# Two-layer encoder trunk with routed experts: small loads placed elsewhere, expert matrices asked for in two steps

## The reference

```
h = RMSNorm(x) * (1 + scale1) + shift1            # scales from SiLU(c) @ ada_w
cols = h @ w_in                                   # split over four mixers A, B, C, D
x = x + gate1 * (concat(A, B, C, D) @ w_out)      # latent, windowed, differential attention, Hyena
h = RMSNorm(x) * (1 + scale2) + shift2
x = x + gate2 * HierMoE(h)
```

## Time and profile before

| | us |
|---|---|
| median of 3 runs | 1742.07 (1737.08 to 1742.08) |
| profiled execution, device time | 1743.41 |
| its span | 1741.6 |
| expert stage, layer 0: first gather issued to last asks after the loop | 574.2 to 862.9 |
| expert stage, layer 1: first gather issued to last result scaled | 1403.6 to 1676.9 |

### The profile page before, as it was taken

The page is one execution under the profiler, slowest core; times in us unless marked ns, Lnnn a source line. Parts: engine busy times, 40 slices in busy tenths (PEclk is TensorE's granted clock), DMA queues, the critical chain, the costliest instruction groups (busy, mean ns, idle before and its releaser), DMA issues.

```text
span 1741.6 us, 18433 instructions
## 1 busy us (share of the span) xinstructions
PE 1382.1 (79%) x6748; PEld 784.0 (45%) x6748; DVE 617.8 (35%) x1444; ACT 369.2 (21%) x832; POOL 266.7 (15%) x250
## 2 busy tenths in 40 slices
PE   2789999898696785888778999989869778877741
PEld 0245646565443443444424464656544344444420
DVE  3462523358624221222136152335761431111111
ACT  0311111545402110111021111154530211111101
POOL 0000310000001342333200030100000134333211
PEclk8799999999898798999978999999989879999976
DMA  7611120441335499999961112045124548999932
GB/s 237 256 46 49 73 88 17 152 176 43 126 124 229 172 286 359 405 404 406 346 241 60 49 63 98 1 147 191 49 105 146 230 161 323 402 402 404 396 134 109
DMA packets 98152, 335.53 MB, mean 193 GB/s; under 512 B 28310, under 2 KB 33046, under 8 KB 72816
## 3 DMA queue, kind: packets, MB, share of 16 engines
q1 hardware_dynamic: 74688, 305.48, 45.0%
q0 software_dynamic: 15072, 16.85, 4.4%
q10 hardware_dynamic: 8304, 12.03, 2.0%
HBM read 324.04 MB, written 27.80 MB: 202 GB/s over the span
## 4 chain that ended last, share of the span: by engine, by line
PE 63%; DVE 14%; issue 9%; ACT 7%; DMA 3%; POOL 2%; SPq 1%; POOLq 0%; DVEq 0%; ACTq 0%
PE bank L468 58%; ACT pr_r L1227 2%; PE bank L716 2%; PE bank L814 2%; DMA big<-in_ada_w_dram 1%; DVE pr_r L1833 1%; DVE pr_r L1694 1%; ACT pr_r L1274 1%; DVE pr_r L1836 1%; DVE pr_r L1559 1%; PE bank L566 1%; POOL small L1334 1%; ACT ht_r L1206 1%; SPq L927 1%; DVE small L1692 1%
## 5 line engine op out<-in xcount | busy, mean ns | idle before, releaser
L468 PE MATMUL bank<-big,pr_r 128*64 128x256 f32 (+2 forms) x3272 | 469.1, 407 | 103.0 <-issue 62.1
L468 PEld LDWEIGHTS bank<-big,pr_r 128*64 128x64 f32 (+1 forms) x3272 | 283.6, 153 | 261.1 <-issue 156.2
L468 PE MATMUL bank<-big,ht_r 128*128 128x512 f32 (+2 forms) x832 | 329.9, 547 | 1.5 <-ACT ht_r L1240 1.5
L468 PEld LDWEIGHTS bank<-big,ht_r 128*128 128x128 f32 x832 | 155.0, 190 | 144.4 <-issue 138.0
L468 PE MATMUL bank<-big 128*128 128x256 f32 (+4 forms) x528 | 191.7, 504 | 28.1 <-ACT big L1211 10.5
L1398 POOL DMA_INDIRECT x_rows<-ht_r,slot_i x64 | 101.7, 1590 | 359.2 <-DVE ht_r L1839 319.7
L468 PEld LDWEIGHTS bank<-big 128*128 128x128 f32 (+2 forms) x528 | 102.2, 205 | 86.1 <-issue 39.9
L1833 DVE TENSOR_TENSOR pr_r<-pr_r,bank 64x256 f32<-64x256 f32 x65 | 27.5, 423 | 291.4 <-ACT pr_r L1274 256.2
L1274 ACT ACTIVATE pr_r<-bank 64x256 f32<-64x256 f32 x64 | 24.1, 377 | 457.3 <-PE bank L468 426.8
L1839 DVE SCALAR_TENSOR_TENSOR ht_r<-bank,mix_r,mod 128x512 f32<-128x512 f32 x65 | 48.8, 751 | 135.9 <-PE bank L468 132.4
L1333 POOL TENSOR_SCALAR small<-small 128x1 f32<-128x1 f32 (+2 forms) x20 | 6.9, 346 | 574.9 <-DVE small L1719 326.6
(11 more groups left out here) (272 smaller groups left out, 1215.7 us busy)
## 6 DMA issues: line engine op xcount, KB each, us to landing
big<-in_moe_w_gate_dram SPq DMA_DIRECT2D x65, 1024.0 KB, 4.9
big<-in_moe_w_up_dram SPq DMA_DIRECT2D x65, 1024.0 KB, 6.9
big<-in_moe_w_down_dram SPq DMA_DIRECT2D x65, 1024.0 KB, 8.9
big<-in_ada_w_dram SPq DMA_DIRECT2D x16, 3072.0 KB
big<-in_w_in_dram SPq DMA_DIRECT2D x4, 3072.0 KB
big<-in_w_out_dram SPq DMA_DIRECT2D x4, 2048.0 KB
mod<-in_ada_b_dram SPq DMA_DIRECT2D x12, 512.0 KB, 5.5
big<-in_w_in_dram SPq DMA_DIRECT2D x2, 2048.0 KB
```

The lines of the kernel that those rows point to most:

```text
L468: return nc.tensor.matmul(o, l, r, start=start, stop=stop)
```

## The change

The loads of the vectors are split in groups with semaphores of their own. In layer 0, those of layer 1 are now issued so: `load_network` (weights, biases and frequencies of the filter network) and `load_conv` (conv weights and bias, the norm vectors, `k_lam`) before chunk 12 (the first half of w_out); `load_attention` (three broadcasts) at expert 2, after the mixers are done; `load_router` at expert 5; `load_filters`, now only its last four DMAs, and `load_mods` at expert 9 as before. Gate and up of expert e are asked for when the gate and up products of the expert before it in the slot are done, its down matrix when all of that expert's products are. The count is read at expert 24 on every engine.

```diff
+READ_AT = 24
...
@@ tensor, first filters of layer 0 (the same split in DVE's wait and at MLP_AT)
-                    pe.wait_ge(hy_in, 16 * 11)
+                    pe.wait_ge(net_in, 16 * 7)
+                    pe.wait_ge(hy_in, 16 * 4)
@@ tensor, before the experts
-                n_over = pe.value_load(tot_i[0:1, 0:1], min_val=0, max_val=EXTRA)
-                n_before = pe.value_load(tot_i[0:1, 1:2], min_val=0, max_val=EXTRA * DEPTH)
-
...
                 for e in range(NE):
                     expert(e)
+                    if e == READ_AT:
+                        n_over = pe.value_load(tot_i[0:1, 0:1], min_val=0, max_val=EXTRA)
+                        n_before = pe.value_load(tot_i[0:1, 1:2], min_val=0, max_val=EXTRA * DEPTH)
@@ sync
+            def load_network(l):
+                (hy_w1, hy_w2, hy_w3, hy_b1, hy_b2, hy_b3, hy_sin_freq: 7 DMAs on net_in)
...
+            def load_conv(l):
+                (hy_conv_w x3, hy_conv_b, mla_q_norm, mla_kv_norm, k_lam: 7 DMAs on vec_in)
...
+            def load_attention(l):
+                (diff_lambda, diff_norm_g, swa_sink: 3 DMAs on vec_in)
...
+            def load_router(l):
+                (router_g_b, router_e_b: 2 DMAs on vec_in)
@@ sync, the chunks of a layer
                     if n == 5:
                         load_late_mods(l)
+                    if CHUNKS[n] == ("out", 0) and l + 1 < DEPTH:
+                        load_network(l + 1)
+                        load_conv(l + 1)
                     chunk_used(sp, CHUNKS[n - 2])
                     load_chunk(n, l)
@@ sync, the experts
                 for e in range(NE):
                     s = EXPERT_SLOT[e]
+                    if e == 2 and l + 1 < DEPTH:
+                        sp.wait_ge(mix_ready, l + 1)
+                        load_attention(l + 1)
+                    if e == 5 and l + 1 < DEPTH:
+                        taken(sp, "lgT")
+                        load_router(l + 1)
                     if before_in_slot(e) is not None:
+                        sp.wait_ge(gu_done, NE * l + before_in_slot(e) + 1)
+                        load_first(e)
                         sp.wait_ge(y_done, NE * l + before_in_slot(e) + 1)
+                        load_down(e)
                     elif s < 2:
...
-                    load_expert(e)
-                    if e == 5:
+                    if before_in_slot(e) is None:
+                        load_first(e)
+                        load_down(e)
+                    if e == READ_AT:
                         taken(sp, "over")
...
                     if e == 9 and l + 1 < DEPTH:
                         load_filters(l + 1)
-                        load_vectors(l + 1)
                         load_mods(l + 1)
@@ scalar and gpsimd: the two value_loads at e == READ_AT, not at e == 4
@@ vector: the two value_loads after the result of expert READ_AT, not before the loop
```

More of the change, by code:

```diff
@@ L265, in trunk @@
         slot_full = [sem(f"slot_full{i}") for i in range(5)]
-        hy_in, vec_in = (sem(n) for n in "hy_in vec_in".split())
+        hy_in, net_in, vec_in = (sem(n) for n in "hy_in net_in vec_in".split())
         x_in = [sem(f"x_in{t}") for t in range(NT)]
@@ L852, in expert @@
                         else:
-                            pe.wait_ge(hy_in, 16 * 11 * (l + 2))
+                            pe.wait_ge(net_in, 16 * 7 * (l + 2))
+                            pe.wait_ge(hy_in, 16 * 4 * (l + 2))
                         mm(bank[4 + b][0:64, :], (hw1, hw2, hw3)[j], mlp_h if j else zT).then_inc(mlp_done, 1)
@@ L909, in load_chunk @@
                     sp.dma_start(at(big, s * SLOT, KT, m), src.rearrange("(p k) n -> p k n", k=KT)).then_inc(slot_full[s], 16)
-            def load_filters(l):
[L913 to L917, removed]
+            def load_network(l):
+                for w, name in ((hw1, "hy_w1"), (hw2, "hy_w2"), (hw3, "hy_w3")):
+                    sp.dma_start(w, of_layer(name, l)).then_inc(net_in, 16)
+                for j, name in enumerate(("hy_b1", "hy_b2", "hy_b3")):
+                    sp.dma_start(hb[:, j:j + 1], row_of(name, l).rearrange("a n -> n a")).then_inc(net_in, 16)
+                sp.dma_start(hf, of_layer("hy_sin_freq", l).rearrange("j n -> n j")).then_inc(net_in, 16)
+            def load_filters(l):
                 sp.dma_start(zT, a["k_z"]).then_inc(hy_in, 16)
@@ L957, in load_empty @@
                 sp.dma_start(slots_of.rearrange("(p n) o -> p (n o)", p=P), a["k_empty"]).then_inc(fill_in, 16)
+            load_network(0)
             load_filters(0)
@@ L962, in _ @@
             load_mods(0)
-            load_vectors(0)
+            load_attention(0)
+            load_conv(0)
+            load_router(0)
             load_chunk(1, 0)
@@ L974, in layer, with load_first @@
                         load_late_mods(l)
+                    if CHUNKS[n] == ("out", 0) and l + 1 < DEPTH:
+                        load_network(l + 1)
+                        load_conv(l + 1)
                     chunk_used(sp, CHUNKS[n - 2])
                     load_chunk(n, l)
-                def load_expert(e):
+                def load_first(e):
                     s = EXPERT_SLOT[e]
-                    wg, wu, wd = expert_slot(s)
+                    wg, wu, _ = expert_slot(s)
                     src = l * NE + TURN[e]
@@ L985, in load_expert, with load_down @@
                         "a (p k) f -> (a p) k f", k=KT)).then_inc(slot_full[s], 16)
-                    sp.dma_start(wd, a["moe_w_down"].rearrange("l e f d -> (l e) f d")[bass.ds(src, 1)].rearrange(
+                def load_down(e):
+                    s = EXPERT_SLOT[e]
+                    src = l * NE + TURN[e]
+                    sp.dma_start(expert_slot(s)[2], a["moe_w_down"].rearrange("l e f d -> (l e) f d")[bass.ds(src, 1)].rearrange(
                         "a (p j) d -> (a p) j d", j=2)).then_inc(slot_full[s], 16)
@@ L1274, in layer @@
                     A_(sil[0:CAP, b, :], bank[2 + b][0:CAP, 0:F], ACT.Silu).then_inc(silu_ready, 1)
-                    if e == 4:
+                    if e == READ_AT:
                         n_over = act.value_load(tot_i[0:1, 0:1], min_val=0, max_val=EXTRA)
@@ L1513, in mod_take @@
                         took(last)
-                v.wait_ge(hy_in, 16 * 11 * (l + 1))
+                v.wait_ge(net_in, 16 * 7 * (l + 1))
+                v.wait_ge(hy_in, 16 * 4 * (l + 1))
                 step(TS(bias_b, bias_b, 2.0 / (2 * S), None, ALU.mult))
@@ L1857, in layer @@
                     y_evac(e % 4, slot_w[:, TURN[e]:TURN[e] + 1]).then_inc(yg_ready, 1)
+                    if e == READ_AT:
+                        n_over = v.value_load(tot_i[0:1, 0:1], min_val=0, max_val=EXTRA)
+                        n_before = v.value_load(tot_i[0:1, 1:2], min_val=0, max_val=EXTRA * DEPTH)
                     if e in MLP_AT and l + 1 < DEPTH:
```

9 lines of the change are left out of this document (3 added, 6 removed).

## The result

The changed kernel takes 1731.09 us, median of 14 runs (1725.47 to 1736.71); the kernel before took 1742.07 (14 runs, 1736.74 to 1749.09; three of them, and its profile, were taken ahead of the prediction). The ratio is 0.9938, 95% interval 0.9924 to 0.9951: 11 us faster. The forecast said faster, by 19.5 us, 1723 with a range of 1713 to 1733. Sign and range held, the range near its slow end; the size was almost twice what came. The profiled execution took 1733.8 us, its span is 1732.0 (before: 1741.6).

What follows compares the result with a forecast made beforehand. The prediction took the DMA engines to bound the expert stages, so gains come from useless DMA time. Terms of 2.1, 9.9 and 7.5 us sum to 19.5 off 1743.41, stated as 1723 us, range 1713 to 1733.

Steps and rivals of the forecast that it cites:

- part 1: Start of both expert stages: removing PE's reads of the count saves 2.1 us in sum, bounds 0 and 2.75.
- in layer 0 I take 1.1, in layer 1 1.0: Before each stage's first transposes: of PE's 1.27 and 1.48 us issue waits, these amounts would be saved.
- Everything in the stage follows from these transposes: Start of each expert stage: the first transposes set all that follows, so the shorter wait counts as gain, 2.1 us.
- Part 2, the asks: Dry queue before expert 7, both layers: earlier gate and up asks gain 5.0 us a stage, 9.9 together, bounds 0 to 16.3.
- fits into the 7.6 us: Layer 0's hole before expert 7: 2.10 MB at 422 GB/s takes 5.0 us, within the 7.6 us by which the ask comes earlier.
- the stall goes too: Rival at expert 3, both layers: ACT's late SiLU start vanishes, the whole hole fills, 6.4 us more gain, 1717; chance 0.1.
- the page weighed against my rate: Refill of the holes: a 358 GB/s HBM bound would make it 5.9 us, worth 1.8 us more; 5.0 was kept.
- Part 3, the small loads: Layer 0, expert 9: moving small loads away from expert 10's asks saves 7.5 us, bounds 2.5 and 9.9.
- the rest, 7.6 us, is what the small loads cost: Layer 0's experts 9 to 31 take 15.7 us longer than layer 1's; remaining loads explain 8.1, moved ones the rest.
- Expert 10's gate and up are asked for by 642: SP in layer 0: with eight loads left at expert 9, the ask comes before 642, with 3.2 MB still queued.
- The cover of chunk 12: Moved loads delay chunk 12's ask from 373.90 to 389 at worst; 90 us of cover makes it free, otherwise 15 us.
- the slower rival, late gathers: Saturated expert stages: gathers sharing full engines arrive late, 26 us lost against 19.5 gained, giving 1749; chance 0.03.

Runs made afterwards that it cites:

- job 3: Four kernels run on one chip, ratios to the kernel before: that kernel unchanged 1.0013, two-step asks alone 0.9979, changed kernel 0.9943, slot order kept 0.9884.
- e1: The kernel before with only the two-step asks (gate and up first, down later): 1739.85 us, ratio 0.9959.
- e4: The changed kernel run once more, on the chip where its three parts were tried singly: 1735.46 us, ratio 0.9931.
- e2: The kernel before with only the small loads regrouped and moved, asks and count as before: 1736.92 us, ratio 0.9940.
- j_asks: The kernel before with only the two-step asks, repeated on another chip: 1738.06 us, ratio 0.9979.
- j_before: The kernel before, with no edit, profiled again on another chip: 1742.83 us, ratio 1.0013.
- j_order: The changed kernel with modulation vectors at expert 5 and slot order 2, 3, 0, 1 kept from expert 5 to 24: 1719.27 us, ratio 0.9884.
- job 1: Four kernels run on one chip, ratios to the kernel before: asks alone 0.9959, small loads alone 0.9940, count alone 0.9990, changed kernel 0.9931.

## Why the prediction was right and where it was wrong

The mechanism held. The saturated rate stayed at 403 to 405 GB/s, and what came off was idle or ill-used DMA time. That the total lay inside the range owes something to its width: its slow end was 10 us of gain. The matched pair of job 3 gives the account. Its spans differ by 1743.8 - 1732.5 = 11.3 us; the stages by 8.1 + 3.2 = 11.3, and what lies around them by 0 in sum (1.6 gained before, 1.2 lost between, 0.5 lost after), so the 1.0 us of part 1, which falls outside the stages, cannot be seen there. One reading of rows was off by a slice or two, and nothing rests on it: the nines of the earlier trace rows are slices 15 to 20 and 35 to 38.

**Part 1, the count on PE: 2.1 forecast, 1.0 measured.** The step that failed is "in layer 0 I take 1.1, in layer 1 1.0". The wait did go, to within 0.1 us in layer 0. But the 32 products behind it ran longer, part of them at the low clock. "Everything in the stage follows from these transposes" overlooked this. The products had been at 5.16 to 5.31 us against the 3.67 us of a warm expert all along. The two bounds, 0 and 2.75, held. At expert 24 the reads cost nothing that shows: the stages of the count alone are 273.6 and 256.6.

**Part 2, the asks: 9.9 forecast, 4.1 to 5.8 measured** (e1 against before 2.6 and 3.2; e4 against e2 2.4 and 1.7; j_asks against j_before 1.7 and 3.0). The step that failed is "fits into the 7.6 us". I took the time of the last product of expert 3 from the trace as the time of its signal. It was the start of SiLU, 2.4 us later, that stood for the signal, and the earlier trace rows showed it: 609.75. With the stall the ask is then 5.1 to 5.3 us early, in which the 5.0 us of transfer would still fit. But the rate in that term was wrong too: 422 GB/s was read behind a long stand of PE, and beside the gathers the refill moves 329 in e1_asks (this row) and 316 in j_asks (above).

```profile
612.00:616.00 4.00, 4.00 (x18) 1.42 (x18) 0.75 (x1) 0.00 (x0) 2.74 (x3) 0.65 0.93 329
```

At 329 GB/s the two matrices need 6.4 us, and the packets of SP's queue put e1_asks only 1.4 and 1.1 MB ahead of the count alone at 30 us. Without the stall the ask comes only 3.7 us sooner than in the kernel before: 17.8 us after expert 0's result in j_asks, 21.5 in j_before. The lead is about what the queue moves in that time, 3.7 x 0.40 = 1.5 MB (the packets say 1.6 and 1.4 MB at 30 us), not the 2.10 MB of the two matrices. That is at most 3.7 us of full rate; 1.7 and 3.0 of it reached the end of the stages. The lead is still some 1.2 and 1.1 MB at 200 us, so the rest was lost among the last experts; how is not shown. The smaller of the matrices' bytes and the interval's bytes would have been an upper bound for the term, not its size. The bounds 0 to 16.3 held.

The rival "the stall goes too", 1717, did not come true as a consequence of the change: the stall came and went between jobs in both kernels. The prediction had read one profile's stall as a property of the program and put it into the interval of 7.6 us.

On the page weighed against my rate (the Trainium skill, "DMA: Bandwidth & Descriptors", section Bandwidth): its sentence on an HBM bound of about 358 GB/s a core does not hold here. The same section of the Trainium skill also says that about 358 GB/s is what each of two cores gets when both stream, and has 425 GB/s as measured with one; this kernel runs on one core. It moved 398 to 406 GB/s from 690 to 800 us in all fourteen profiles, and the profile shows 324 MB read from HBM in a run, of the 336 MB that the queues moved. The measurement decides, and the sum was right to go by the rows.

**Part 3, the small loads: 7.5 forecast, 6.4 measured** (273.1 to 266.7 alone, 6.9 against the count alone of the same job; 268.8 to 262.4 beside the asks). The step is "the rest, 7.6 us, is what the small loads cost". The mechanism is right, the term a sixth too large. In the changed kernel layer 0 is still 262.4 - 251.1 = 11.3 us above layer 1, and the 3.2 MB that stay explain 8.1 of it. With the modulation vectors gone and the order kept it is 253.8 - 247.3 = 6.5, of which the filters' 1.1 MB explain 2.8. So 3 to 4 us of the difference of the layers are more than these loads' bytes at full rate. Some 2 us of that are most likely still theirs: the 8 and 10 us from 632 on move 325 and 372 GB/s in layer 0 of j_order, at a share of 1.05, and 389 and 401 in layer 1 at the same distance from expert 0's result (from 1438 on), 0.8 MB more. So 8.1 us, bytes over full rate, was too little for the loads that stay, and the 7.6 us left too much for those that move. The last 1 to 2 us stay open. Layer 0 also asks for the next layer's first chunk and the waves before its last experts are done, but behind expert 31's matrices; nothing was tried on it.

Two side claims fared as follows. "Expert 10's gate and up are asked for by 642": it was 645.35, since four large broadcasts held SP for 12.7 us, where the prediction had some 4 us for all but the bias. "Its transfer is then continuous": yes, 340 GB/s at a share of 1.05, a little under the 350 named. The cover of chunk 12 held with its ask at 378.87, ten us sooner than the worst case of 389. Of the slower rival, late gathers, nothing was seen: no piece of the chain waits for one behind expert 0 in any of the fourteen profiles, and the saturated stretches move 398 to 406 GB/s from 690 to 800 us and 400 to 405 from 1500 to 1610. (The 398 and 400, at the prediction's sign of 400, are those of the kept slot order, whose stages are the shortest.)

The sum by measured parts is 1.0 + 4.7 + 6.4 = 12.1, where the total time gives 11.0 (interval 8.5 to 13.2) and the matched pair 11.3.

## What to carry to other kernels

Where a queue runs dry because an ask waits for an engine, an earlier ask is worth at most the interval it gains times the rate, and no more than its bytes; here, without the stall, 4.7 us came of it in two stages where that bound is 7.4. The moment of a signal is read at the engine that it wakes: it was 0.1 us from the row of the next matmuls without the stall, and 2.3 us with it. A stage bound by DMA gains most when bytes leave it for a time when the queue is empty: 2.1 MB moved from expert 9 to expert 5 gave 5.4 us, about as much as the asks in two steps on both layers. Take both profiles of a pair from one job, and compare them stage by stage, before a difference of one per cent is explained.

## What the runs showed of the hardware that I had not expected

- The same program can have a stall of 2.3 to 2.5 us at one place in one job and not in another. The changed kernel has it in job 1 (below, layer 0) and not in its first profile, where these transposes waited 0.26 us, nor in job 3; there its stages are 1.9 and 3.3 to 4.4 us shorter.

```profile
607.77 0.75 PE L799 MATMUL bank<-ident,ht_r 128*128 128x128 f32 x4
610.84 0.45 PE L813 MATMUL bank<-ident,pr_r 64*128 64x64 f32 x2 [2.32 <-issue]
```

- Work that starts 1 us sooner after PE has stood still can take 0.5 us longer (5.66 us for 5.16), with the mean granted clock at 0.63 in place of 0.69. PE in front of its first expert shows a granted clock of 0.50 in the changed kernel:

```profile
570.00:580.00 10.00, 4.80 (x32) 4.51 (x32) 6.26 (x27) 0.00 (x0) 0.19 (x1) 0.50 0.00 0
```

- A few broadcast loads can hold the issuing engine far longer than their number suggests: three modulation DMAs took 6.8 to 10.3 us to issue at expert 9 behind a filled queue, in the five profiles of kernels with the moved loads that ask for them there, and 1.41 us at expert 5, where this row is from.

```profile
561.50 1.41 SPq L953 DMA_DIRECT2D mod<-in_ada_b_dram  x3
```
